# Nine weight slabs of each attention layer rounded by ScalarE instead of GpSimd

## The reference, cut to what matters

```python
def diff_attention(h, w_in, lam, subln, w_out, rel_bias, layer_idx):
    q, k, v = jnp.split(h @ w_in, [DA_QK, 2 * DA_QK], axis=-1)      # 8 heads, two maps each
    for blk in range(S // BLOCK):                                  # 4 blocks of 128 queries
        s = jnp.einsum('bmqd,bmkd->bmqk', q[:, :, qs:ke], k[:, :, :ke])
        a = jax.nn.softmax(where(rel >= 0, s + bias, -inf))
        a = a[:, :, 0] - lam_full * a[:, :, 1]
        outs.append(jnp.einsum('bhqk,bhkv->bhqv', a, v[:, :, :ke]))
    o = rms_norm(o, subln) * (1.0 - lam_init)                       # per head
    return o @ w_out
```

## Time and profile before

| | |
|---|---|
| median of 3 runs | 3572.69 us (3572.06 to 3575.16) |
| the profiled execution's own time | 3573.81 us |
| its span, first to last instruction | 3572.0 us |
| mean granted TensorE clock | 0.997 of full speed |
| busy over the span | TensorE 98%, VectorE 49%, ScalarE 27%, GpSimd 18% |

### The profile page before, as it was taken

One profiled execution on the slowest core, in us unless ns is written; L12 is line 12 of the kernel. 1 busy time (PEld: TensorE's weight loads), 2 busy tenths in 40 slices (PEclk: granted clock), 3 DMA queues, 4 the chain that ended last, 5 costly groups with the idle time before them and its releaser, 6 DMA issues.

```text
span 3572.0 us, 44203 instructions
## 1 busy us (share of the span) xinstructions
PE 3511.2 (98%) x18378; PEld 2949.6 (83%) x18378; DVE 1762.2 (49%) x2257; ACT 961.6 (27%) x1679; POOL 630.9 (18%) x369
## 2 busy tenths in 40 slices
PE   8999999999999999999999999999999999999999
PEld 6778888888888888688888877888888888898887
DVE  4455334647653346663335445553464446663434
ACT  2652001324220013641003265210141215120102
POOL 2103111200031112021112111311121111111110
PEclk9999999999999999999999999999999999999999
DMA  5312222222122223122222321222222222222222
GB/s 204 107 60 95 96 101 87 100 95 86 63 95 95 100 89 109 60 79 101 98 95 83 112 83 60 98 95 96 93 71 96 82 95 95 103 98 94 94 95 71
DMA packets 65463, 332.88 MB, mean 93 GB/s; under 512 B 9795, under 2 KB 20291, under 8 KB 28532
## 3 DMA queue, kind: packets, MB, share of 16 engines
q1 hardware_dynamic: 44316, 303.50, 23.8%
q10 hardware_dynamic: 20952, 26.56, 2.3%
HBM read 326.22 MB, written 10.90 MB: 94 GB/s over the span
## 4 chain that ended last, share of the span: by engine, by line
PE 87%; DVE 6%; ACT 5%; issue 1%; POOL 1%; DMA 1%; DVEq 0%; ACTq 0%; POOLq 0%
PE proj L496 23%; PE proj L498 23%; PE proj L497 23%; PE proj L617 2%; PE proj L618 2%; PE proj L619 2%; PE proj L529 2%; PE proj L530 1%; PE proj L531 1%; DVE wlo L1730 1%; PE mix L691 1%; DVE s L1838 1%; ACT h L1159 1%; ACT xh L1156 1%; PE mix L717 1%
## 5 line engine op out<-in xcount | busy, mean ns | idle before, releaser
L467 POOL TENSOR_SCALAR whi<-raw 128x2048 fp32r<-128x2048 f32 x273 | 531.0, 1945 | 2712.9 <-DVE wlo L1730 1758.3
L496 PE MATMUL proj<-gh,whi 128*128 128x512 f32 x1968 | 785.1, 399 | 12.5 <-ACT gh L1108 10.5
L498 PE MATMUL proj<-gh,wlo 128*128 128x512 f32 x1968 | 770.7, 392 | 0.0
L497 PE MATMUL proj<-gl,whi 128*128 128x512 f32 x1968 | 769.8, 391 | 0.0
L1730 DVE TENSOR_TENSOR wlo<-raw,whi 128x2048 fp32r<-128x2048 f32 x286 | 653.4, 2285 | 147.6 <-POOL whi L467 104.8
L496 PE MATMUL proj<-xh,whi 128*128 128x512 f32 x1760 | 695.4, 395 | 8.8 <-DVE wlo L1730 3.1
L497 PE MATMUL proj<-xl,whi 128*128 128x512 f32 x1760 | 688.6, 391 | 0.0
L498 PE MATMUL proj<-xh,wlo 128*128 128x512 f32 x1760 | 688.5, 391 | 0.0
L496 PEld LDWEIGHTS proj<-gh,whi 128*128 128x128 f32 x1968 | 370.7, 188 | 106.3 <-issue 15.6
L498 PEld LDWEIGHTS proj<-gh,wlo 128*128 128x128 f32 x1968 | 370.3, 188 | 80.8
L497 PEld LDWEIGHTS proj<-gl,whi 128*128 128x128 f32 x1968 | 370.8, 188 | 78.6 <-issue 1.9
(11 more groups left out here) (312 smaller groups left out, 4279.9 us busy)
## 6 DMA issues: line engine op xcount, KB each, us to landing
raw<-in_stream SPq DMA_DIRECT2D x286, 1024.0 KB, 4.8
da_b<-bias_da ACTq DMA_DIRECT2D x16, 512.0 KB, 3.5
bias_da<-bias_rows ACTq DMA_DIRECT2D x8, 512.0 KB, 10.5
h<-in_x ACTq DMA_DIRECT2D x4, 512.0 KB, 8.8
bias_sw<-bias_table ACTq DMA_DIRECT2D x1, 2048.0 KB, 9.9
pf<-in_p ACTq DMA_DIRECT2D x4, 512.0 KB, 7.0
sw_b<-bias_sw ACTq DMA_DIRECT2D x4, 512.0 KB, 3.5
out_features<-fin SPq DMA_DIRECT2D x8, 256.0 KB, 2.5
```

Of the source, the lines that this page charges most:

```text
L467: nc.gpsimd.tensor_scalar(whi[SLOT[n]][:, :, :], raw[SLOT[n]][:, :, :], 1.0, 0.0, ALU.mult, ALU.add).then_inc(hi_done, 1)
L496: nc.tensor.matmul(out, wh, ah, start=first, stop=False, skip_group_check=check)
L497: nc.tensor.matmul(out, wh, al, start=False, stop=False, skip_group_check=check)
L498: return nc.tensor.matmul(out, wl, ah, start=False, stop=last, skip_group_check=check)
```

## The change

In the two attention layers the high parts of slabs s0+6 to s0+14 move from GpSimd to ScalarE. ScalarE makes the high part of s0+6+i directly behind the i-th of the nine copies, so in the rounds 3, 6, 9, 12, 15, 18, 20, 23 and 26, ahead of `head_hi` and `at_copy`. VectorE's low parts stay where they are and now wait for ScalarE. `high_part` is moved up from the layer 1 mixer so that both can call it.

```diff
+            def high_part(n):
+
+                if n in ACT_SLABS:
+                    act.wait_ge(raw_in[SLOT[n]], LANDED[n])
+                    A(whi[SLOT[n]][:, :, :], raw[SLOT[n]][:, :, :], ACT.Copy).then_inc(*own.sig(hi_act))
+
             def da_mixer(d, layer):
...
                     if k - 1 in DA_FILLED:
                         i = DA_FILLED.index(k - 1)
                         evac(i // 3 + 1, i % 3)
+                        high_part(s0 + 6 + i)
                     if k >= 7 and k % 4 == 3:
                         head_hi((k - 7) // 4)
...
-ACT_SLABS = list(range(PLAN.at["mix1"][0] + 5, PLAN.at["mix1"][0] + 18))
+ACT_SLABS = [PLAN.at[f"mix{layer}"][0] + j for layer, first, end in ((0, 6, 15), (1, 5, 18), (3, 6, 15)) for j in range(first, end)]
```

More of the change, by code:

```diff
@@ L1298, in values_back @@
                     act.dma_start(hg_v[:, g % 2, :, P:2 * P], turned_v[2 + g % 2].rearrange("(t p) n -> p t n", p=P)).then_inc(M("v_back"), 16)
[L1300 to L1304, removed]
                 def far_copy(g):
```

## The result

The changed kernel takes 3579.24 us, the median of 16 runs (3576.38 to 3583.13). The kernel before took 3572.95 us in the 16 runs beside them (3570.67 to 3575.53). The ratio is 1.0019, with a 95% interval of 1.0012 to 1.0026: 6.3 us more, between 4.3 and 9.3. The forecast was 3579.2. The prediction's line between slower and no change, 0.2%, lies inside the interval of 0.12% to 0.26%, so this comparison doesn't tell on which side of it the change is; that it costs something is clear.

The account below looks back on a forecast made before the run. TensorE was taken to bound the kernel, ending last for 87% of the span. Losses of 3.35 us in layer 3 and 3.15 in layer 0, together 6.5, gave 3579.2 us against the median of 3572.69, range 3574 to 3586.

Parts of the forecast that it names:

- The removal: Eighteen GpSimd high parts of 1945 ns go; worth nothing, as VectorE never waits for them; a 0.73 us port hold is hidden.
- The added instruction: Eighteen on ScalarE, nine per layer, 1916 ns each in layer 1; each holds what follows by 1.82 us, no table load.
- Round 3: Mask starts 3.4 us late behind the low part; 0.6 us of slack before TensorE's next scores, so no loss.
- Rounds 12, 15, 20 and 23: VectorE's side keeps about 1 us or more of slack before the scores; these rounds lose nothing.
- Round 7: High part in round 6 delays post_sq, for which the next round's mean_square waits; loss 0.3 us per layer.
- Round 11: Round 9's late low part delays mask, exps, at_copy and post_sq, then mean_square; loss 0.75 us in layer 3, 0.55 in layer 0.
- Round 19: High part in round 18 delays at_copy and post_sq, so mean_square starts late; loss 0.5 us per layer.
- Round 27: High part in round 26 stands ahead of at_copy and post_sq without slack; the whole 1.82 us is lost per layer.
- Hidden: Rival: unseen waits cover part of the mean_square delays, only round 26 counts or less; 3572.7 to 3576.3 us; chance 0.17.
- Faster: Rival: without nine GpSimd high parts VectorE is never held at the shared port, 0.73 us a hit; chance 0.03.
- VectorE's queue decides: Rival: scores also wait for the mask in rounds 4, 10 and 19; 4 to 8 us on top, 3585 us; chance 0.1.
- The clock falls: Rival: the 1.7 us wait in round 27 lowers TensorE's clock, 0.8 to 1.5 us more per layer, 3581.5 us; chance 0.2.

Follow-up runs that it names:

- Experiment 2: Against the kernel before, ScalarE makes only the high parts of rounds 3, 12, 15, 20 and 23 in each attention layer: 3572.72 us, ratio 1.0000.
- double dose: The changed kernel with each of ScalarE's high parts in the attention layers made twice: 3608.24 us, ratio 1.0099 against the kernel before.
- experiment 3: The changed kernel with VectorE's low parts one round later, except the last: 3576.01 us, ratio 1.0009 against the kernel before.
- experiment 1: The changed kernel with the last high part of each attention layer (round 26) back on GpSimd: 3574.80 us, ratio 1.0007 against the kernel before.
- experiment 7: The kernel before with only the last of the nine high parts per layer (round 26) on ScalarE: 3575.52 us, ratio 1.0007.
- experiment 8: The changed kernel with the copies of rounds 15 and 23 ahead of second and exps: 3570.88 us, ratio 0.9994 against the kernel before.
- experiment 6: The kernel before, high parts on GpSimd, with the copies (da_k) of rounds 15 and 23 ahead of second and exps: 3564.07 us, ratio 0.9974.
- experiment 5: The double dose: the changed kernel with each of ScalarE's attention-layer high parts made twice: 3608.24 us, ratio 1.0099 against the kernel before.

## Why the prediction was right

The mechanism came as it was worked out, place by place. That 3579.24 us lies so close to the forecast of 3579.2 is luck: the waits are 0.5 us smaller than the sum, and the interval alone is 5 us wide.

**The removal was worth nothing.** Experiment 2 takes ten of eighteen high parts from GpSimd and stays at 1.0000. The hold on VectorE was there and went: `da_a` of round 0 in layer 3, 1.08 us beside GpSimd's high part in the earlier trace rows, takes 0.35 in the profile after, with nothing on GpSimd beside it.

```profile
2027.51 0.35 DVE L2008 SCALAR_TENSOR_TENSOR da_a<-da_s,small,da_t 128x128 f32<-128x128 f32 x1 [0.47 <-ACT da_t L1230]
```

This agrees with the rule of the Trainium skill (SBUF — State Buffer, Who interferes with whom). The 0.73 us stayed in VectorE's slack, and none of TensorE's waits in the loops went with it.

**The added instruction.** Its 31 instances in the profile after have a median of 1900 ns, and it holds ScalarE by 1.80 us where 1.82 was taken. The Trainium skill (ScalarE: Activation LUTs, What ACT_TABLE_LOAD costs) gives 186 ns plus 0.833 ns an element, an estimate of 1892 ns for 2048, with an overlap of 93 ns; the trace agrees, with 1900 ns and, from the rows of round 26, 100 ns. No table load was added: the ones in rounds 26 and 27 are those of `head_std`.

**Round 3, no loss.** This was the tightest place. The low part starts at 2043.17, right behind the high part, and the mask follows it:

```profile
2041.24 1.90 ACT L1189 ACTIVATE whi<-raw 128x2048 fp32r<-128x2048 f32 x1
...
2043.17 2.29 DVE L1731 TENSOR_TENSOR wlo<-raw,whi 128x2048 fp32r<-128x2048 f32 x1 [3.50 <-ACT whi L1189]
...
2045.85 0.28 DVE L1988 CUSTOM_DVE_ANT_0 da_s<-mix,da_b 128x128 f32<-128x128 f32 x1
...
2046.68 0.70 PE L691 MATMUL mix<-da_k,da_q 64*128 64x256 f32 x4
```

The mask ends at 2046.13 and the scores start at 2046.68 without a wait: 0.55 us of slack, where 0.6 was worked out. In seven of the nine rounds of each layer VectorE waits for the high part, as forecast, and no scores wait for it.

**Rounds 12, 15, 20 and 23, nothing.** Right, by experiment 2 and by the list of waits. "About 1 us or more" of slack on VectorE's side was a little generous: in the double dose, with some 1.9 us more of delay, scores wait 1.15 us (layer 3) and 0.80 us (layer 0) for the mask of round 21, which leaves an estimate of 0.75 to 1.1 us.

**The four losses.** Round 7: 0.3 was worked out, 0.19 and 0.18 measured. Round 11: 0.75 (layer 0: 0.55), measured 0.82 (0.64), and through the mask, as experiment 3 shows. Round 19: 0.5, measured 0.38 twice. Round 27: 1.8, measured 1.71 twice. The sum was 6.5 and is 6.0. The terms of rounds 7, 19 and 27 are about 0.1 too large each. ScalarE was held 1.80 us and not 1.82, and `mean_square` started 0.64 us behind `post_sq` and not 0.67. Counted from the start of the copy, `mean_square` of layer 3 comes 0.26, 0.44 and 1.77 us later than before; why the waits of the rows are 0.06 to 0.07 less than that isn't shown. One small thing was missed: in layer 0 the wait for `post_on` in round 27 grew from 0.7 to 1.0.

**The parts don't add up exactly.** Experiments 1 and 7 split the change into +2.0 and +2.7, 4.7 together, where the change measured +6.3 and experiment 8 against 6 measured +6.8. By their waits they should give 2.6 and 3.4. Each of them has an interval of some 3 us to either side, so this is within the measurement, and by its time alone neither is told from no change. TensorE's idle time in the profiles does add up: 2.9 us more in experiment 1 and 3.5 in experiment 7, 6.4 together, and 6.8 in the change.

**The rivals.** *Hidden* fell: all four places show in the trace. *Faster* fell with the change's own time, whose interval lies above 1. *VectorE's queue decides* did not come about, for no scores wait for a mask that did not before; the point from which it decides was right, since in the double dose scores wait 1.4 us for the mask of round 4. *The clock falls* is the one that is partly true. It was put as a yes or no for the wait of 1.7 us in round 27. What the runs show is that the same wait has it in one execution and not in the next: yes in layer 0 of experiment 7, no in its layer 3 and no in both layers of the change's profile, in all in one case of eight. At up to 1.5 us a case, the prediction's price, that is an estimate of 0.4 us for both layers. Eight cases are few, and the comparison by mean clock leaves 5.6 to 7.9 us for the whole change, so the clock's mean share in the 6.3 us stays open; only profiles of many executions could settle it.

## What to carry to other kernels

The busy share says where there is room for work, and not whether it is there at the moment: ScalarE was busy 27% of the span, but 58% of the loop in which the work was put (116.44 of 202.00 us in the earlier trace rows), and every round had an instruction right behind the insertion that TensorE wanted at once or a bit later. So read the busy share in the stretch where the work will stand. Before moving work to such an engine, write down for each place what stands behind it in that engine's queue, when it is wanted, and how much of the delay its slack takes; here that gave 0 for ten moves and 6.5 us for eight, whose waits measured 6.0. And read the waits of the bottleneck engine that the change does not touch: the 5.7 us of waiting for a copy that stood behind `second` and `exps` were worth 8.7 us (5.7 to 12.5), as much as the whole change cost, 6.3 (4.3 to 9.3), or more.

## What the hardware showed

TensorE's clock fell to the lower of its two levels behind waits well under 2 us, and not each time. The waits of 1.77 us for `da_k` had it in one execution (0.50 in the earlier trace rows) and not in another (1.00 at the same place after the change), in all in 11 cases of 16; the waits of 1.71 us for `post_sq` in one of eight; and in the double dose it stayed up behind waits of 2.33 us. The scatter goes with it: runs of one kernel at a mean clock of 0.996 lie 3 to 5 us over those at 0.998. For this reason a short wait can be worth more than its length. Taking away 5.7 us of waits gave 8.7 us (experiment 6), with 2.6 us less of busy time in its profile, and the double dose, with 24.1 us more of idle time, gave 35.5 (experiment 5), with 10.8 us more of busy time.
